# A decoder layer in fp32 on one core: the norm's factor moved behind the projections, the first weight block in four transfers, the key rotation behind the index sums

## The reference, cut to what matters

```
xn = x * rsqrt(mean(x*x) + eps) * g                    # RMSNorm, per token and per channel
q, k, v, iq, ik, iw, u, qm = split(xn @ w_in)          # one combined projection, 2632 columns
q, k, iq, ik = partial_rope(...)                       # the first 16 of each 64 columns are rotated
index: sum over 8 heads of relu(iq @ ik.T / 8) * iw, causal; the best 64 keys per token are kept
y_attn = softmax attention on these keys; y_pool = causal pooling of u; y_mem = attention of qm into memory tokens
gates = sigmoid(xn @ w_gate + b_gate)                  # 3 * 1024 columns
h = x + (sum over the branches of gate * (y @ w_proj)) @ w_out
h = h + MoE(RMSNorm(h))                                # top 4 of 32 experts, clamped SwiGLU
out = RMSNorm(h)
```

## Time and profile before

| | |
|---|---|
| median of 3 runs | 1175.01 us |
| the profiled execution: its own time | 1175.06 us |
| its span | 1173.3 us |
| TensorE busy | 1105.7 us (94%) |
| VectorE / ScalarE / GpSimd busy | 346.8 / 234.6 / 146.1 us |
| bytes moved | 444.25 MB, 379 GB/s over the span |

### The profile page before, as it was taken

One profiled execution on the slowest core, in us unless ns is written; L12 is line 12 of the kernel. 1 busy time (PEld: TensorE's weight loads), 2 busy tenths in 40 slices (PEclk: granted clock), 3 DMA queues, 4 the chain that ended last, 5 costly groups with the idle time before them and its releaser, 6 DMA issues.

```text
span 1173.3 us, 14340 instructions
## 1 busy us (share of the span) xinstructions
PE 1105.7 (94%) x5713; PEld 510.5 (44%) x5713; DVE 346.8 (30%) x755; ACT 234.6 (20%) x427; POOL 146.1 (12%) x67
## 2 busy tenths in 40 slices
PE   7989999999999999999999999999999899899996
PEld 7869999853333333333333333333333233233332
DVE  3584475332222222222222222222222222222222
ACT  5444554421111111111111111111111111111112
POOL 5852767700000000000000000000000000000000
PEclk9999999999999999999999999999999999999999
DMA  9654345999999999999999999999999999999994
GB/s 354 229 194 160 144 147 173 392 415 382 420 428 428 428 428 427 427 428 427 428 428 428 427 427 426 428 428 427 427 428 428 426 427 428 428 428 428 428 427 165
DMA packets 50248, 444.25 MB, mean 379 GB/s; under 512 B 6110, under 2 KB 9608, under 8 KB 25608
## 3 DMA queue, kind: packets, MB, share of 16 engines
q1 hardware_dynamic: 48272, 441.64, 90.4%
q10 hardware_dynamic: 1912, 1.66, 0.5%
HBM read 441.65 MB, written 1.05 MB: 377 GB/s over the span
## 4 chain that ended last, share of the span: by engine, by line
PE 61%; DMA 29%; DVE 6%; ACT 3%; issue 1%; POOL 0%; ACTq 0%; SPq 0%; DVEq 0%
PE psum L1536 23%; PE psum L1572 15%; DMA ring<-in_w_up 15%; PE psum L1217 14%; DMA gm_area<-in_w_up 10%; DMA my_area<-in_w_up 4%; PE psum L1488 3%; DVE gate_area L1146 1%; DVE gate_area L1142 1%; DVE gate_area L1140 1%; PE psum L1559 1%; ACT gate_area L802 1%; PE psum L1545 1%; PE psum L1292 1%; PE psum L1314 1%
## 5 line engine op out<-in xcount | busy, mean ns | idle before, releaser
L1536 PE MATMUL psum<-ring,gate_area 128*64 128x512 f32 x1216 | 278.6, 601 | 20.6 <-DMA ring<-in_w_up 13.1
L1112 DVE TENSOR_TENSOR h_s<-psum,h_s 128x512 f32<-128x512 f32 x132 | 81.9, 682 | 427.4 <-PE psum L1488 427.4
L1536 PEld LDWEIGHTS psum<-ring,gate_area 128*64 128x64 f32 x1216 | 85.2, 138 | 202.4 <-issue 170.4
L1572 PE MATMUL psum<-ring,gate_area 128*64 128x512 f32 x640 | 145.8, 595 | 5.3 <-ACT gate_area L802 5.3
L565 POOL TENSOR_TENSOR unit_lo<-ring,unit_hi 128x1024 fp32r<-128x1024 f32 (+1 forms) x57 | 133.6, 2350 | 80.9 <-ACT unit_hi L598 80.8
L796 ACT ACTIVATE gate_area<-gate_area 128x512 f32<-128x512 f32 x32 | 20.1, 629 | 530.1 <-DVE gate_area L1138 530.1
L1138 DVE TENSOR_SCALAR gate_area<-psum 128x512 f32<-128x512 f32 x32 | 22.1, 691 | 273.7 <-PE psum L1545 273.7
L1572 PEld LDWEIGHTS psum<-ring,gate_area 128*64 128x64 f32 x640 | 44.3, 136 | 86.3 <-issue 76.3
L598 ACT ACTIVATE unit_hi<-ring 128x1024 fp32r<-128x1024 f32 (+1 forms) x57 | 58.5, 1034 | 45.2 <-PE psum L1217 43.5
L1488 PE MATMUL psum<-pT_s,gate_area 64*128 64x512 f32 x264 | 65.6, 615 | 0.7 <-ACT pT_s L806 0.7
L806 ACT ACTIVATE pT_s<-psum 128x512 f32<-128x512 f32 x32 | 19.1, 597 | 221.7 <-PE psum L1572 221.7
(11 more groups left out here) (240 smaller groups left out, 1190.4 us busy)
## 6 DMA issues: line engine op xcount, KB each, us to landing
ring<-in_w_up SPq DMA_DIRECT2D x76, 2048.0 KB, 37.1
ring<-in_w_down SPq DMA_DIRECT2D x40, 2048.0 KB, 38.1
qe_area<-in_w_up SPq DMA_DIRECT2D x16, 2048.0 KB, 37.2
gm_area<-in_w_up SPq DMA_DIRECT2D x16, 2048.0 KB, 39.0
my_area<-in_w_up SPq DMA_DIRECT2D x12, 2048.0 KB, 34.2
xv_area<-in_w_up SPq DMA_DIRECT2D x8, 2048.0 KB, 37.6
xv_area<-in_w_down SPq DMA_DIRECT2D x8, 2048.0 KB, 40.3
my_area<-in_w_down SPq DMA_DIRECT2D x8, 2048.0 KB, 43.2
```

The source lines that it names most:

```text
L1112: nc.vector.tensor_tensor(h_s[:, b, cols], psum[:, BACK_BANKS[j], :], h_s[:, b, cols], ALU.add).then_inc(added, 1)
L1536: ins = nc.tensor.matmul(psum[lo:lo + SLOTS, c, :], lhsT, w[:, at:at + 512], start=(k == 0), stop=False)
L1572: ins = nc.tensor.matmul(psum[c * SLOTS:(c + 1) * SLOTS, DOWN_BANK, :], lhsT, w[:, at:at + 512], start=(f == 0), stop=(f == KC - 1))
```

## The change

The input is turned as it arrives, without the factor r. The factor is applied where the products leave PSUM: VectorE multiplies by it when it empties block A, ScalarE does so when it empties IQ, Q, K and V (`copy_scaled`). For QM and the gates, whose tokens lie along the columns, a tile `rstd_bc` with r along the columns is made: VectorE multiplies the identity by r (`diagonal`, two instructions), TensorE multiplies it by ones (job `rstd`, between the memory tokens and block Q), VectorE copies it out. VectorE then multiplies each gate and `qmT` by this tile, and ScalarE takes the tanh in place. Block A is loaded by four transfers between those of x. On ScalarE the squares of x and of the memory tokens stand between the splits of units 4 to 8, and the split of unit 19 stands behind head 5. On VectorE the rotation of k stands behind the index sums. Nine matmuls on ones that filled TensorE's time ahead of the turning are gone.

```diff
@@ sync
-            for b in range(B):
-                sp.dma_start(h_s[:, b, :], x[0, b * P:(b + 1) * P, :]).then_inc(got_x[b], 16)
+            sp.dma_start(h_s[:, 0, :], x[0, 0:P, :]).then_inc(got_x[0], 16)
+            sp.dma_start(first_block[:, 0:2, :], win[:, 0:2, C_IK:C_QM]).then_inc(got_first[0], 16)
+            sp.dma_start(h_s[:, 1, :], x[0, P:S, :]).then_inc(got_x[1], 16)
+            sp.dma_start(first_block[:, 2:4, :], win[:, 2:4, C_IK:C_QM]).then_inc(got_first[1], 16)
+            sp.dma_start(first_block[:, 4:6, :], win[:, 4:6, C_IK:C_QM]).then_inc(got_first[2], 16)
+            sp.dma_start(first_block[:, 6:8, :], win[:, 6:8, C_IK:C_QM]).then_inc(got_block[0], 16)
@@ scalar
-            for b in range(B):
-                act.wait_ge(got_x[b], 16)
-                ins = squares_of(h_s, 0, b)
-            link(ins)
-            root(0)
+            split(0)
...
+            split(3)
             split(4)
+            nc.scalar.activation(warm[:], eps_s[:], ACT.Sqrt)
+            squares_of(h_s, 0, 0)
+            split(5)
+            link(squares_of(h_s, 0, 1))
+            root(0)
+            split(6)
             act.wait_ge(got_mem, 16)
             squares_of(mem_s, 8, 0)
+            split(7)
             link(squares_of(mem_s, 8, 1))
             root(8)
-            for u in range(5, 11):
+            for u in range(8, 11):
                 split(u)
...
+            def copy_scaled(name, b, dst):
+                nc.scalar.activation(dst, empty((name, b)), ACT.Copy, scale=st[:, 6 + b:7 + b]).then_inc(act_emptied, 1)
...
                 nc.scalar.activation(relu_s[:, h % 2, :], t[:, 0:P + S], ACT.Relu, scale=HD ** -0.5)\
                   .then_inc(act_emptied, 1)
+                if h == 5:
+                    split(19)
...
             def gate(m):
-                t = empty(("gate", m))
-                nc.scalar.activation(gates[:, m, :], t[:, 0:S], ACT.Tanh, bias=gate_b[:, m:m + 1], scale=0.5)\
-                  .then_inc(act_emptied, 1)
                 u = 22 + m + UNIT_SLOTS
                 if u < len(UNITS):
                     split(u)
+                act.wait_ge(dve_emptied, EMPTIED["gate", m])
+                nc.scalar.activation(gates[:, m, :], gates[:, m, :], ACT.Tanh, bias=gate_b[:, m:m + 1], scale=0.5)\
+                  .then_inc(gates_ready, 1)
@@ vector
-            scale_rows(xn_area, h_s, 0, 1)
...
-            scale_rows(mem_s, mem_s, 8, 2)
+            inverse_rms(0, 1)
...
+            scale_rows(mem_s, mem_s, 8, 2)
+            dve.wait_ge(got_ident, 16)
+            for b in range(B):
+                nc.vector.tensor_scalar(diagonal[:, b, :], ident[:], st[:, 6 + b:7 + b], None, ALU.mult)\
+                  .then_inc(diagonal_set, 1)
...
-            for b in range(B):
-                dve.wait_ge(act_emptied, EMPTIED["K", b])
-                rotate(k_s, b, HEADS)
...
             link(nc.vector.tensor_tensor(idx[:, 2 * P:3 * P], idx[:, 2 * P:3 * P], causal[:], ALU.add))
+
+            for b in range(B):
+                dve.wait_ge(act_emptied, EMPTIED["K", b])
+                rotate(k_s, b, HEADS)
...
+            def scale_gate(m):
+                t = empty(("gate", m))
+                nc.vector.tensor_tensor(gates[:, m, :], t[:, 0:S], rstd_bc[:], ALU.mult).then_inc(dve_emptied, 1)
@@ tensor
-            keep_busy(psum[:, 7, :], 9)
-            transposes("xT", xn_area, scaled, 1)
+            transposes("xT", h_s, [(got_x[b], 16) for b in range(B)])
...
+            t = fill("rstd")
+            pe.wait_ge(diagonal_set, B)
+            for b in range(B):
+                ins = nc.tensor.matmul(t[:, b * P:(b + 1) * P], ones[:], diagonal[:, b, :], start=True, stop=True)
+            done(ins)
```

More of the change, by code:

```diff
@@ L116, in psum_jobs @@
     jobs += [(("IQ", b), "act") for b in range(B)]
-    jobs += [(("memT", j), "dve") for j in range(4)]
+    jobs += [(("memT", j), "dve") for j in range(4)] + [("rstd", "dve")]
     jobs += [(("Q", b), "act") for b in range(B)]
@@ L127, in psum_jobs @@
     for m in range(PAIRS):
-        jobs += [(("gate", 4 * m + i), "act") for i in range(2)]
+        jobs += [(("gate", 4 * m + i), "dve") for i in range(2)]
         jobs += [(("pT", 2 * m + i), "act") for i in range(2)]
@@ L131, in psum_jobs @@
             jobs += [(("sc", 2 * m + 2 + i), "act" if m + 1 < MPAIRS else "dve") for i in range(2)]
-            jobs += [(("gate", 4 * m + 2 + i), "act") for i in range(2)] + [(("o", m), "dve")]
+            jobs += [(("gate", 4 * m + 2 + i), "dve") for i in range(2)] + [(("o", m), "dve")]
         else:
-            jobs += [(("gate", 4 * m + 2), "act"), (("o", m), "dve"), (("gate", 4 * m + 3), "act")]
+            jobs += [(("gate", 4 * m + 2), "dve"), (("o", m), "dve"), (("gate", 4 * m + 3), "dve")]
     for f in range(KC):
@@ L313, in hybrid_layer_kernel @@
         pooledT = view(pT_s, 0, G // 2, S)
+        diagonal = view(pT_s, 0, B, P)
         relu_s = lg_s
@@ L364, in hybrid_layer_kernel @@
         ones_set = sem("ones_set")
+        got_first = [sem(f"got_first{i}") for i in range(3)]
+        diagonal_set = sem("diagonal_set")
+        gates_ready = sem("gates_ready")
         hi_ready = sem("hi_ready")
@@ L620, in _ @@
                 ins.then_inc(xT_hi_ready, 1)
-                if j == 1:
-                    split(0)
-            for u in range(1, 4):
-                split(u)
+                if j < 2:
+                    split(j + 1)
+            split(3)
             split(4)
+            act.wait_ge(got_eps, 1)
+            nc.scalar.activation(warm[:], eps_s[:], ACT.Sqrt)
[4 more added lines that the diff above has]
+            split(6)
             act.wait_ge(got_mem, 16)
             squares_of(mem_s, 8, 0)
+            split(7)
             link(squares_of(mem_s, 8, 1))
             root(8)
-            for u in range(5, 11):
+            for u in range(8, 11):
                 split(u)
@@ L666, in _ @@
                 act.dma_start(b_rows[rows_of, 512:768], b_down[0][:, 256 * q:256 * q + 256]).then_inc(got_bias, 16)
-            for u in range(19, 23):
+            for u in range(20, 23):
                 split(u)
             for b in range(B):
-                copy(("V", b), v_s[:, b, :])
+                copy_scaled("V", b, v_s[:, b, :])
             split(23)
@@ L994, in take_o @@
                 nc.vector.tensor_tensor(lo, t[:, 0:S], hi.bitcast(F32), ALU.subtract).then_inc(dve_emptied, 1)
+            def scale_gate(m):
+                t = empty(("gate", m))
+                nc.vector.tensor_tensor(gates[:, m, :], t[:, 0:S], rstd_bc[:], ALU.mult).then_inc(dve_emptied, 1)
+            t = empty("qmT")
+            for c in range(2):
+                ins = nc.vector.tensor_tensor(qmT[:, c, :], t[:, c * S:(c + 1) * S], rstd_bc[:], ALU.mult)
+            ins.then_inc(dve_emptied, 1)
             bias_parts()
@@ L1195, in transposes @@
                         for b in range(B):
-                            if j == 0 and c == 0 and count_sem is not None:
-                                pe.wait_ge(count_sem, count + b)
+                            if j == 0 and c == 0:
+                                pe.wait_ge(*arrived[b])
                             ins = nc.tensor.transpose(t[:, c * S + b * P:c * S + (b + 1) * P],
@@ L1239, in _ @@
             project("IQ", 512)
-            transposes("memT", mem_s, scaled, 3)
+            transposes("memT", mem_s, [(scaled, b + 1) for b in range(B)])
+            t = fill("rstd")
[3 more added lines that the diff above has]
+            done(ins)
             project("Q", 512)
```

53 lines of the change are left out of this document (35 added, 18 removed).

## The result

The changed kernel takes 1180.91 us, the median of 6 runs (1179.15 to 1183.95), beside 1174.76 for the kernel before in the same session, also 6 runs: a ratio of 1.0048, 95% interval 1.0036 to 1.006. It is slower, by half a percent. The profiled execution took 1179.59 us with a span of 1177.8, 4.5 us longer than the span of before, 1173.3.

A forecast was written before the change was run, and what follows sets the result against it. It took the expert loop as bound by the weight stream, which starts when the front ends, so each front microsecond counts. 2.4 + 0.8 + 2.8 + 1.6 = +7.6 on 1175.06 gave 1182.7, predicted as 1182.5, range 1173 to 1187.

The forecast's parts named there:

- The start: Blocks A and IQ: A starts some 4 us earlier, IQ lands unchanged at 17.8; gain at most 1.7 us.
- The chain behind it: Ahead of block Q: GpSimd passes hold VectorE's scalings and diagonals, TensorE waits, Q starts at 39.1; +2.4 us net.
- the stall before Q: TensorE ahead of block Q: stands 3.1 us until VectorE's two diagonals are done.
- the bounds of -1.7 to +3.5: Block Q's shift: -1.7 us if nothing is held, +3.5 if every term is late by half a pass.
- The clock there: Behind the stall before Q: lower granted clock costs between 0 and 1.7 us, taken as +0.8.
- The index sums and what is late next: Blocks V to QM: V ends 4.0 us earlier, but held sums and rotation delay `mix` 6.8 us; +2.8.
- The bound of sums that aren't held: Ahead of `mix`: sums of heads 6 and 7 pass beside GpSimd, stall 0; chance 0.25, shared with a half-stall case.
- The clock behind that wait: Behind the stall of 6.8 us ahead of `mix`: lower granted clock on TensorE costs +1.6 us.
- The gates: Gate loops: 24 more VectorE multiplications, 0.42 us each, 10 us in all, fit beside its work; cost 0.
- the index part: Index sums to QM, with rotation of k and split of unit 19 moved: +2.8 us, and +1.6 of clock.
- the early chain: Work up to block Q: +2.4 us from held VectorE instructions and +0.8 us of clock.

The follow-up runs named there:

- e9: e8 with 18 matmuls on ones between blocks A and IQ on TensorE; 1174.87 us, ratio 0.9993 to the kernel before.
- e3: Changed kernel with the split of unit 19 put back behind the transfers of the biases; 1175.52 us, ratio 1.0 to the kernel before.
- e1: Changed kernel with the emptying of pooling moved ahead of the rotation of k on VectorE; 1175.9 us, ratio 0.9996 to the kernel before.
- e10: Kernel before with split of unit 19 behind head 5, pooling emptied first, rotation of k behind both selections; 1172.41 us, ratio 0.9973.
- e4: Changed kernel with both index changes undone (rotation of k and split of unit 19 as before); 1177.87 us, ratio 1.0018 to the kernel before.
- e6: Kernel before with one edit, the split of unit 19 behind head 5; 1172.84 us, ratio 0.9979.
- e8: e1 with the rotation of k behind both top-64 selections on VectorE; 1173.71 us, ratio 0.999 to the kernel before.

## Why the prediction was right, and where it was not

It gave 1182.5 us, slower, within 1173 to 1187; measured 1180.91. By its steps, in the profiled execution:

- *The start.* IQ landed 12.91 us after its turn in the queue at 4.92, at 17.83 (forecast 17.8), and unit 4 came at 21.53 (forecast 21.3). Right: IQ was issued 1.2 us later than before (3.69) and landed when it did before, and block A's 4.3 us went into a wait.
- *The chain behind it*, +2.4 (39.1 against the trace's 36.68; against its own reconstructed 36.9 it would be 2.2). This step failed: measured 36.21 - 36.68 = -0.47. The sum took TensorE through IQ as if at full clock and GpSimd "without a break". I had noted what a wait does to the clock, and used it for the stall before Q, not for the longer one before IQ. There it came, and put the gap of 0.16 us between two passes in which the second diagonal went. e9 shows the step's own mechanism when the clock is kept: 2.58 us of wait, Q at 38.16, 1.5 us later than before. Both values lie inside the bounds of -1.7 to +3.5 that the prediction gave; which of them holds hangs on the clock behind IQ's wait.
- *The clock there*, +0.8: measured 0 before Q. It was paid inside IQ, within the term above.
- *The index sums and what is late next*, -4.0 + 6.8 = +2.8. Right: `mix` starts 82.16 - 79.75 = 2.41 later, and 0.47 more against an earlier Q, +2.88. The wait was 6.49 (6.8 forecast), the held sum 2144 ns ("about 2 us"). That the wait fits so well is in part luck: the pass of unit 20 was to begin with three of the eight instructions through; it began about half a us earlier than that, against block Q, with none through, and the five left over behind the three passes took longer by as much. The bound of sums that aren't held is excluded; e3 and e1 show the two links, the pass that holds the sum and the emptying behind the rotation.
- *The clock behind that wait*, +1.6: measured 91.12 - 82.16 = 8.96 from `mix` to the product with `memT`, before 86.61 - 79.75 = 6.86, so +2.1. The 1.6 leaned on the 1.7 worked out for the wait of 2.80 us; e10, where the lower clock is absent behind that wait, puts its loss at 1.2 (Q at 35.48 against 36.68).
- *The gates*, 0. Right: 422 ns each, TensorE busy 140.00 of 140.00 us. The factor on `qmT` isn't in the sum, which puts it at 0; that holds only while QM is late, as e1 shows.

The sum is then -0.47 + 2.88 + 2.1 = 4.5 where 7.6 was forecast. The sign came out because the larger terms stood in the index part; the early chain was mis-sized by 3.7 us with its clock. The median of the runs lies 6.15 us above that of before, the profiled span 4.5. The second profiled execution of the changed kernel took longer, 1181.15 us with a span of 1179.4: its expert loop starts at 252.99, as in the first (253.03), and the 1.6 us more lie behind that, in the loop. So the front makes 4.4 us of the loss in both. That a forecast of +7.6 lies near the 6.15 of the medians owes something to what the loop adds, for which the prediction has no term; what brings that about stays open.

## What to carry to other kernels

Where GpSimd runs long passes, count every VectorE instruction that reads two SBUF operands or is a tensor-scalar in SBUF as one per pass where the passes follow each other without a gap, and put what TensorE waits for ahead of them, not behind: moving one emptying of 0.69 us ahead of eight such instructions brought the next block 7.4 us forward. Then look what is late next: half of that gain over the kernel before was gone at the scores. When a wait appears or goes, carry the clock's loss and the new pace of the other engines through the sum before the next step is judged; two losses can hide each other. And when a change bundles several edits, look for the one that gains: here the split of unit 19, moved ahead by two heads, gave 0.2% alone, and the rotation behind the sums took back more.

## What the runs showed of the hardware

- The granted clock after a wait isn't a function of its length in these runs. Behind 2.12 us (before) and 2.05 us (e3) it stayed 1.00, behind 2.26 us (e4) it fell to 0.50; behind the 2.79 us ahead of block A it was 0.50 and 0.65 in e6 and 1.00 in e10; behind 4.5 us it fell each time, and block Q came between 36.15 and 37.46 in seven executions. Ahead of the expert loop, behind a wait of 0.67 us and a row of small products, it fell to 0.50 in e1 and stayed 1.00 in the kernel before.
- The instructions of the selections aren't held: MAX8 and MATCH_REPLACE8, with one full operand in SBUF, took 0.28 us each at 74.83 and 75.23 in e8, inside three passes from 74.25 to 81.36. A tensor-scalar that reads PSUM isn't either: block A's emptying at 24.07 in the changed kernel took 0.48 us inside passes from 22.54.
- An instruction that gets its turn when a pass ends runs into the next one and delays it. In the changed kernel the two scalings end 0.24 and 0.32 us behind the starts of the passes at 29.99 and 32.71, and these show 2.48 and 2.56 us where an undisturbed one shows 2.35 to 2.39. In e9, without a gap, the first scaling ends 0.59 us behind the start of the pass at 29.55, which shows 2.86.
